# Two attention stages of a decoder kernel: paired heads, two groups in flight, and DVE scaling before it takes maxima

## What is computed

```python
s = jnp.einsum('bkgnqd,bknsd->bkgnqs', q_blk, k_band)      # k_band: 16 meta keys, previous block, own block
s = jnp.where(mask, s, NEG_INF)
m = jnp.maximum(jnp.max(s, axis=-1, keepdims=True), sink)
p = jnp.exp(s - m)
p = p / (jnp.sum(p, axis=-1, keepdims=True) + jnp.exp(sink - m))
o_real = jnp.einsum('bkgnqs,bknsd->bkgnqd', p, v_band)     # 16 heads, dim 64, 2 query blocks of 128
```

## Time and profile before

| | |
|---|---|
| Runs shown | 1983.89, 1986.37, 1986.67 us; median 1986.37 us |
| The profiled execution | 1978.87 us, span 1976.8 us |
| TensorE busy | 1835.7 us (93%) |
| DVE busy | 1089.6 us (55%) |
| ACT busy | 774.6 us (39%) |
| Mean granted TensorE clock | 0.955 |
| The chain that ended last | PE 80%, DVE 13%, ACT 3% |

### The profile page before, as it was taken

One profiled execution on the slowest core, in us unless ns is written; L12 is line 12 of the kernel. 1 busy time (PEld: TensorE's weight loads), 2 busy tenths in 40 slices (PEclk: granted clock), 3 DMA queues, 4 the chain that ended last, 5 costly groups with the idle time before them and its releaser, 6 DMA issues.

```text
span 1976.8 us, 33553 instructions
## 1 busy us (share of the span) xinstructions
PE 1835.7 (93%) x12950; PEld 1513.3 (77%) x12950; DVE 1089.6 (55%) x2037; ACT 774.6 (39%) x1225; POOL 23.2 (1%) x31
## 2 busy tenths in 40 slices
PE   6999979889999999977889999999889999999995
PEld 5999969689999999965589998999774444444442
DVE  3775566677755876483367756665863222222224
ACT  4554442355545544443355445765421111111111
POOL 1000000000000000000000001000020000000000
PEclk9999999999999999996599999999899999999998
DMA  6555324034553455520035555344269999999993
GB/s 171 190 180 200 123 86 154 18 131 175 180 196 126 160 180 205 179 86 1 1 121 183 185 205 171 138 150 148 86 247 397 420 421 420 421 420 421 420 421 153
DMA packets 55469, 409.60 MB, mean 207 GB/s; under 512 B 6368, under 2 KB 6368, under 8 KB 7904
## 3 DMA queue, kind: packets, MB, share of 16 engines
q1 hardware_dynamic: 53424, 401.69, 53.6%
q0 software_dynamic: 1680, 5.78, 0.9%
q10 hardware_dynamic: 288, 1.05, 0.1%
HBM read 405.87 MB, written 2.63 MB: 207 GB/s over the span
## 4 chain that ended last, share of the span: by engine, by line
PE 80%; DVE 13%; ACT 3%; issue 2%; DMA 1%; ACTq 0%; SPq 0%; DVEq 0%
PE ps L537 78%; PE ps L541 2%; DVE w_lo L1482 2%; DVE h L1589 1%; DVE h L1585 1%; DMA par<-params 1%; DVE x_lo L1544 1%; ACT w_hi L1130 1%; DVE rs L1524 1%; DVE arena L1842 0%; DVE arena L1917 0%; DVE small L1847 0%; DVE arena L1766 0%; DVE moe L2179 0%; ACT moe L1426 0%
## 5 line engine op out<-in xcount | busy, mean ns | idle before, releaser
L537 PE MATMUL ps<-x_hi,w_hi 128*128 128x256 f32 (+1 forms) x2144 | 623.9, 291 | 32.6 <-DVE w_lo L1482 19.9
L537 PE MATMUL ps<-x_lo,w_hi 128*128 128x256 f32 (+1 forms) x2144 | 616.5, 288 | 0.0
L537 PE MATMUL ps<-x_hi,w_lo 128*128 128x256 f32 (+1 forms) x2144 | 614.3, 287 | 0.0
L1482 DVE TENSOR_TENSOR w_lo<-raw,w_hi 128x1024 fp32r<-128x1024 f32 (+1 forms) x352 | 440.6, 1292 | 89.9 <-ACT w_hi L1130 89.7
L537 PEld LDWEIGHTS ps<-x_hi,w_hi 128*128 128x128 f32 x2144 | 409.9, 191 | 47.6 <-issue 19.9
L1130 ACT ACTIVATE w_hi<-raw 128x1024 fp32r<-128x1024 f32 (+1 forms) x352 | 378.1, 1110 | 91.9 <-PE ps L537 72.1
L537 PEld LDWEIGHTS ps<-x_hi,w_lo 128*128 128x128 f32 x2144 | 411.9, 192 | 0.0
L537 PEld LDWEIGHTS ps<-x_lo,w_hi 128*128 128x128 f32 x2144 | 411.2, 192 | 0.2
L537 PE MATMUL ps<-ring,moe 128*64 128x512 f32 x1536 | 336.9, 594 | 0.8 <-ACT moe L1419 0.8
L537 PEld LDWEIGHTS ps<-ring,moe 128*64 128x64 f32 x1536 | 107.6, 137 | 205.0 <-issue 201.2
L537 PE MATMUL ps<-hid_hi,w_hi 128*128 128x272 f32 (+1 forms) x720 | 206.0, 286 | 0.6 <-DVE hid_lo L1544 0.2
(11 more groups left out here) (312 smaller groups left out, 1982.0 us busy)
## 6 DMA issues: line engine op xcount, KB each, us to landing
raw<-w_units SPq DMA_DIRECT2D x144, 1024.0 KB, 4.8
ring<-w_gate_up SPq DMA_DIRECT2D x128, 1024.0 KB, 12.8
ring<-w_down SPq DMA_DIRECT2D x64, 1024.0 KB, 12.1
raw<-w_out_units SPq DMA_DIRECT2D x32, 1408.0 KB, 5.9
bias_rows<-arena POOLq DMA_DIRECT2D x8, 192.0 KB, 2.6
cst<-table SPq DMA_DIRECT2D x1, 1448.0 KB, 21.5
h<-xT SPq DMA_DIRECT2D x1, 1088.0 KB, 5.2
arena<-bias_rows POOLq DMA_DIRECT2D x8, 128.0 KB, 2.4
```

The costliest lines, as they stand in the source:

```text
L537: return nc.tensor.matmul(out_ap, lhsT, rhs, start=start, stop=stop, skip_group_check=True)
L1482: v.tensor_tensor(part(w_lo, c, 0, n), raw_slot(u, j * n, n), part(w_hi, c, 0, n).bitcast(F32), ALU.subtract).then_inc(lo_made, 1)
```

## The change

In all three `attend` functions:

- Scores of a head go into one bank, both query blocks behind each other (416 columns in the sliding-window stage, 384 in MoBA); two banks per group. TensorE issues them piece by piece, the two heads beside each other.
- TensorE runs scores two groups ahead (scores(0), scores(1), then scores(g+2), turns of g, outputs of g-1), in both stages.
- Transposes fill three banks a group (512 columns, 256 columns, 512 columns of the 16 meta rows), in MoBA two; ACT copies them with three (two) instructions in place of eight (four).
- Outputs go in the order block, piece, head, in place of block, head, piece.
- DVE scales and masks a head with one instruction of 416 columns (MoBA still two). It runs maxima(0), maxima(1), normalise(0), and then per round normalise(g+1), maxima(g+2), and in MoBA finish_head(g).
- ACT takes exponents(0), and then per round exponents(g+1), the copies of group g, the outputs of g-1.
- The probabilities have three sets of buffers in place of two, the transposed ones two sets in both stages.

```diff
-            def attend(names, groups, first, pb, pitch, pT, q_of, k_of, v_of, segs, done, lag=0):
+            def attend(names, groups, first, pbs, pTs, second, row, q_of, k_of, v_of, segs, turns, done):
...
                 def scores(g):
                     done(g)
-                    for u in range(4):
-                        n, b = divmod(u, 2)
-                        t = S.at(4 * g + u)
+                    ts = [S.at(2 * g + b) for b in range(2)]
+                    banks = [free(t) for t in ts]
+                    for n in range(2):
+                        for at, size, key in segs[n]:
+                            for b in range(2):
+                                hs = slice(64 * b, 64 * b + 64)
+                                c = n * second + at
+                                m = mm(banks[b][:, c:c + size], q_of(g, hs, n), k_of(g, hs, key, size), True, True)
...
                 def outputs(g):
...
+                    for n in range(2):
+                        for s, (at, size, key) in enumerate(segs[n]):
+                            for b in range(2):
+                                a = t_at[2 * n + b, s]
+                                m = mm(bank[64 * b:64 * b + 64, n * P:(n + 1) * P], v_of(g, b, key, size),
+                                       pTs[g % 2][0:size, a:a + P], s == 0, s == len(segs[n]) - 1)
...
                 scores(0)
+                scores(1)
                 for g in range(groups):
-                    if g + 1 < groups:
-                        scores(g + 1)
...
+                    if g + 2 < groups:
+                        scores(g + 2)
+                    turns_of(g)
+                    if g:
+                        outputs(g - 1)
+                outputs(groups - 1)
```

```diff
+                exponents(0)
+                for g in range(groups):
+                    if g + 1 < groups:
+                        exponents(g + 1)
+                    if g >= 2:
+                        act.wait_ge(full[V.at(g - 2)[0]], V.at(g - 2)[1] + 1)
+                    base = 0
+                    for i, (rows, cols, parts) in enumerate(turns):
+                        t = TT.at(len(turns) * g + i)
+                        nc.scalar.activation(pTs[g % 2][0:rows, base:base + cols], filled(t)[0:rows, 0:cols], ACT.Copy)\
+                            .then_inc(evac[t[0]], 1)
+                        base += cols
+                    if g:
+                        outputs(g - 1)
+                outputs(groups - 1)
```

```diff
                 maxima(0)
+                maxima(1)
+                normalise(0)
                 for g in range(groups):
                     if g + 1 < groups:
-                        maxima(g + 1)
-                    at = 16 + (g % 2) * 16
-                    dve.wait_ge(exp_made, first + g + 1)
...
+                        normalise(g + 1)
+                    if g + 2 < groups:
+                        maxima(g + 2)
                     if between is not None:
                         between(g)
```

More of the change, by code:

```diff
@@ L44 @@
 MAXB = NE + 2 * SEQ // SLOTS
+SWA_ROW = P + SEQ + 2 * META
+MOBA_ROW = P + SEQ
 RAW = 2
@@ L236, in two_blocks @@
         s_o = room(KT * SEQ)
-        a_p = room(2 * 4 * TA)
-        a_pT = room(2 * 4 * 384)
+        a_p = [room(2 * SWA_ROW) for _ in range(3)]
+        a_pT = [room(1280) for _ in range(2)]
         place[0] = 0
@@ L253, in two_blocks @@
         b_rows = room(2 * 512)
-        b_pT = arena[:, place[0] - 2 * 1024:place[0] - 2 * 1024 + 4 * 384]
+        b_pT = [arena[:, place[0] - 2 * 1024 + i * 768:place[0] - 2 * 1024 + (i + 1) * 768] for i in range(2)]
+        b_ps = [b_p[:, 0:2 * MOBA_ROW], b_p[:, 2 * MOBA_ROW:4 * MOBA_ROW], b_att[:, 0:2 * MOBA_ROW]]
         place[0] = 0
@@ L838, in outputs @@
                     bank = free(t)
[L839 to L846, removed]
+                    taken(TT.at(len(turns) * (g + 1) - 1))
@@ L1305, in _, with attend, exponents @@
             split_to(plan["sq"][0] + 4)
-            def attend(names, groups, first, pb, pitch, pT, widths, n_full, meta, o, sinks, lag=0):
+            def attend(names, groups, first, pbs, pTs, second, row, turns, o, sinks):
                 S, TT, V = (plan[x] for x in names)
-                def outputs(g):
-                    t = V.at(g)
-                    nc.scalar.activation(o[:, g * SEQ:(g + 1) * SEQ], filled(t)[:, 0:SEQ], ACT.Copy).then_inc(evac[t[0]], 1)
-                for g in range(groups):
-                    at = 16 + (g % 2) * 16
+                def exponents(g):
+                    at = 16 + (g % 3) * 16
                     act.wait_ge(neg_max, first + g + 1)
@@ L1326, in attend @@
-                    for u in range(4):
-                        t = TT.at(4 * g + u)
-                        bank = filled(t)
-                        if g > lag:
-                            act.wait_ge(full[V.at(g - 1 - lag)[0]], V.at(g - 1 - lag)[1] + 1)
-                        n = n_full[u // 2] * P
-                        a = (g % (1 + lag) * 4 + u) * 384
-                        c = nc.scalar.activation(pT[:, a:a + n], bank[:, 0:n], ACT.Copy)
-                        if meta:
-                            c = nc.scalar.activation(pT[0:META, a + n:a + n + P], bank[0:META, n:n + P], ACT.Copy)
-                        c.then_inc(evac[t[0]], 1)
@@ L1337, in attend, with outputs @@
-                    if g >= lag:
-                        outputs(g - lag)
-                if lag:
-                    outputs(groups - 1)
-            attend(("ss", "sT", "sv"), 8, 0, a_p, TA, a_pT, (P + META, SEQ + META), (1, 2), True, s_o, True,
-                   lag=1)
+                    e.then_inc(exp_made, 1)
+                def outputs(g):
+                    t = V.at(g)
+                    nc.scalar.activation(o[:, g * SEQ:(g + 1) * SEQ], filled(t)[:, 0:SEQ], ACT.Copy).then_inc(evac[t[0]], 1)
@@ L1855, in maxima, with normalise @@
                             .then_inc(neg_max, 1)
-                maxima(0)
-                for g in range(groups):
-                    if g + 1 < groups:
-                        maxima(g + 1)
-                    at = 16 + (g % 2) * 16
+                def normalise(g):
+                    at = 16 + (g % 3) * 16
                     dve.wait_ge(exp_made, first + g + 1)
```

101 lines of the change are left out of this document (61 added, 40 removed).

## The result

| | before | after |
|---|---|---|
| Median of the runs | 1985.38 us (1983.89 to 1986.67) | 1930.04 us (1928.12 to 1933.83) |
| Ratio, 95% interval | | 0.9724 [0.9709, 0.974] |
| The profiled execution | 1978.87 us, span 1976.8 | 1929.93 us, span 1927.8 |
| Mean granted TensorE clock | 0.955 | 0.966 |
| Sliding-window stage, first scores to the projection | 108.01 us | 56.63 us |

Measured again, the change took 1930.25 us (1929.68 to 1932.24), ratio 0.9726 [0.9712, 0.9741]. The forecast was 1933.9, its range 1926 to 1944.

The account below looks back on a forecast made before the run. Half-clock TensorE bounded 11 of 13.9 us per sliding-window group, with DVE exposed in the rest. Saving 52.0 us there plus 0.5 in MoBA, 52.5 off the 1986.37 median, gave 1933.9 us, range 1926 to 1944.

Parts of the forecast that it names:

- What bounds the stage: Sliding-window stage after the change: normalise 1.44, maxima 2.7 and exponentials 2.05 make 6.2 us per group.
- The start: Sliding-window stage: normalise(0) starts at 884.7, normalise(1) at 886.8, normalise(7) at 924.0 us.
- Outputs: Sliding-window TensorE outputs: paired heads overlap, five steps and four height changes, 3.0 us at half clock, 1.5 at full.
- Scores: Sliding-window TensorE scores: three wide steps of 0.43 plus some 0.4 for meta parts, 1.7 us at half clock.
- The rule on loads: Scores' weight loads: skill page's 107 ns each, twenty in a row 2.1 us, slow end some 2 us later.
- The clock: TensorE in the sliding-window stage: alternates, end between 929.5 (fast) and 936.9 (slow), middle 933.2 taken.
- MoBA: Second attention: 0.5 us saved (-1 to +2); 1.17 wait goes, about 0.6 comes, up to 1.5 lost at low clock.
- The sum: Whole kernel: 52.0 us from the sliding-window stage plus 0.5 from MoBA, 52.5 us saved.
- Loads one after another: Rival, chance 0.12: sliding-window scores stay at 2.9 us, 42.8 us saved, 1943.6 us.
- no overlap: Rival, chance 0.08: paired heads do not overlap, only fewer drains; outputs 5.0, scores 2.9, 1959.6 us.
- drains: Rival, chance 0.03: alternating heads drain the array each time, 14.8 us a round, 1992.2 us.
- Two groups in flight: Rival, chance 0.02, that they do not take hold: 2.95 us gap stays in seven rounds, near 1955 us.

Follow-up runs that it names:

- against the second: The kernel before, unchanged, profiled a second time: 1986.93 us, span 1984.8.
- the heads apart: The changed kernel with scores and outputs issued one head after the other, normalise still first: 1933.06 us, ratio 0.9735 to before.
- matmuls in all gaps: The changed kernel plus unread matmuls ahead of sliding-window transposes, eight for the first group, three for each other: 1927.92 us, ratio 0.972 to before.

## Why the prediction was right, point by point

- **What bounds the stage.** Normalise 1.44, maxima 2.7 and exponentials 2.05 were summed to a round of 6.2 us; it is 6.23, with 2.08 us of DVE's wait in it. That this loop is the bound, and not TensorE beside it, is shown three ways: TensorE 6.10 in place of 4.15 us at full clock, with the round unmoved; full clock for 41 us, with the round unmoved; and the wait taken out by order, with the round at 4.15.
- **The start.** Normalise(7) was put at 924.0 in the time of the trace before, whose stage starts at 877.18: 46.8 us behind its start. It came 47.1 behind (925.83 - 878.74).
- **Outputs.** 3.0 us at half clock were forecast, 2.92 measured; at full 1.5 and 1.69. The price of a change of height does not halve with the clock: 0.19 us at half, 0.15 at full. The Trainium skill, page "TensorEngine Tiling (Array Packing)", section "Key Properties", says that a change of tiling mode drains the engine. If the step between 128 and 16 rows is such a change, these two numbers are what it costs here; the runs show the times and not the draining.
- **Scores: the term of the sum that was mis-sized.** "3 x 0.43 for the wide steps and some 0.4 for two pairs of meta parts": 1.7 us at half clock, 0.85 at full. Measured: 2.25 and 1.22. Single loads of the trace of after show which part it was (each row is from a window that holds one load of each head; the first two at full clock, the last two at half):

```profile
905.83 0.20 PEld L555 LDWEIGHTS ps<-kT,arena 64*128 64x128 f32 x2
...
905.94 0.20 PEld L555 LDWEIGHTS ps<-kT,arena 64*128 64x128 f32 x2
...
913.51 0.34 PEld L555 LDWEIGHTS ps<-kT,arena 64*128 64x128 f32 x2
...
913.72 0.34 PEld L555 LDWEIGHTS ps<-kT,arena 64*128 64x128 f32 x2
```

Two loads take 0.34 us together, where one alone takes 0.33 (at 926.72 in the trace of before): the two heads, in different row halves, run wholly beside each other. But each head's loads start 0.21 us apart at half clock and 0.11 at full, and so do those of the meta keys (905.83, 905.94 and 913.51 are theirs), whose matmuls have 16 columns but whose weights have 128 like the others. So a meta step costs what a wide one does: five steps of 0.43 and 0.1 for the end make the 2.25. The 0.4 was too small because the 2.91 us of before were read as free of overlap. They were not: the second head's loads, though issued behind the first's, run beside them from 927.14 on. It cost little: the slow TensorE round is 2.3 + 2.92 + 2.25 = 7.5 in place of 7.0. TensorE fell behind DVE twice, at the start (transposes at 891.65, 3.24 us behind normalise(1), where 0.85 is the least) and from 909 to 922 (1.82 us behind at 915.17), and caught up at full clock both times.
- **The rule on loads.** By the Trainium skill (page "TensorE: Matmul & The Clock Gate", section "LDWEIGHTS (loading the stationary operand)") a load takes its column count over 1.2 GHz, an estimate of 107 ns for 128 columns, and twenty in a row would take 2.1 us. That this lies near the 2.25 us measured is luck: ten loads follow one another in each head, the two heads' at the same time. The 0.11 us from load to load at full clock agrees with the page, the 0.21 us at half clock is twice its figure; all these loads are f32, and the measurement decides.
- **The clock.** It alternated, as expected, and the stage's length of 56.63 us lies between the fast end (929.5 - 877.18 = 52.3) and the slow one (59.7), at 56.0 for the value taken. It had also been at full level twice in the trace of before, and not once as the prediction read it (1.00 in 889.3 to 892.7 and in 896.1 to 902.9). What I did not see is why it ends slow: TensorE waits 2.2 us ahead of the last transposes and the clock is at half from there to 940.
- **MoBA.** 0.5 us forecast; the fourth x tile comes 1.62 us sooner, and 0.62 are left behind the projection's slow start, as told with the result. The loss at low clock that the prediction named (up to 1.5 us) did come, about 1 us. But the two traces differ by more than 0.62 us where nothing was edited: right, and not shown apart from chance. The wait that was to come (0.6 or a little more) is 0.80, and the 1.17 is gone.
- **The sum.** 52.5 us forecast; 51.4 to 53.5 for the stage, 0.6 for MoBA, and 55.3 between the medians. The last 1 or 2 us are within the runs' spread. Between the spans of single traces it is 49.0 (against the first of before) or 57.0 (against the second), so no single pair settles the sum to better than some 4 us.
- **The rivals.** Loads one after another asked for 2.9 us of scores (they do follow one another, but in each head for itself), no overlap for 5.0 of outputs, drains for 14.8 a round; each falls by the rows above. Two groups in flight did take hold: at half clock TensorE is busy 13.00 of the 13.00 us from 909 to 922, where it had idled 2.95 in each 13.94.

What the prediction did not say, though its own sum held it, is that the order of normalise and maxima was the dearest part of the change. It named the wait, priced it at 2.05 us a round, and did not ask what the other order would give: 18 us less.

## What to carry to other kernels

With more groups in flight, look on each in-order engine for a step whose input is made on another engine from the step right ahead of it; put another group's step between the two. Here that exchange of two calls, maxima(g+2) ahead of normalise(g+1), gives 1912 us (1912.76 beside the change's 1930.25) and beats both kernels. And price an edit only in the schedule in which it will run: two heads side by side were worth 26 us, at most some 3, or 17, as the loop beside them left it.

## What was not expected of the hardware

- More TensorE work left the clock higher: with the heads apart the whole run's mean clock is 0.975, the change's 0.966, and the stage 59.0 us in place of 56.6 for 7 us more of matmul time (54.5 us busy against 47.4). Most of what was added was given back.
- Filling TensorE's gap at the start of the stage, with maxima first, only moved the fall of the clock from 887 to 893 us: it came behind the next gap, of 1.26 us ahead of the transposes at 892.71. The length of the last gap alone does not tell when it falls. The change's fall at 909 came with a gap of 1.73 us; in its second trace two gaps of 1.74 us stand ahead of 901.98 and of 908.22, and only with the second the clock fell; and with matmuls in all gaps there was no fall in 41 us, one gap of 1.90 us ahead of 922.19 included; it fell with the next one of that length, ahead of 928.43. What decides stays open.
- Heads in different halves of the array run wholly beside each other when their pieces alternate. In column halves (outputs) heads one after the other do not overlap, and the time went from 5.79 to 2.92 us at half clock, 0.76 of it for the four changes of height saved. In row halves (scores) they overlap in part even then, so that less was left to gain: 2.91 to 2.32 us.
- A matmul of 16 columns whose weights have 128 took the step of a wide one, 0.21 us at half clock and 0.11 at full: in the scores the loads set the pace, not the columns.
